# Half-size seven-product blocks in two feed-forward up phases, and split parts of the hidden tensors made in the down phases

## The reference

```python
def swiglu_ffn(x, w_in, w_out):            # feed-forward 0 and 1
    gate, up = jnp.split(x @ w_in, 2, axis=-1)
    return (jax.nn.silu(gate) * up) @ w_out
...
def conv_ffn(x, w_up, conv_w, conv_b, w_down):   # feed-forward 2 and 3
    up = x @ w_up
    a, g = up[..., :D_FF_2], up[..., D_FF_2:]
    g = causal_dwconv(g, conv_w) + conv_b
    return (jax.nn.gelu(g) * a) @ w_down
```

## Time and profile before

| what | value |
|---|---|
| median of three runs | 2401.6 us |
| the profiled execution | 2402.46 us |
| its span, first to last instruction | 2400.6 us |
| mean granted TensorE clock | 0.998 of 2.4 GHz |
| PE busy | 2385.5 us (99%) |
| DVE, ACT, POOL busy | 1094.6, 806.7, 65.3 us |
| DMA engines, mean share | 27.7% |

### The profile page before, as it was taken

The page is one execution under the profiler, slowest core; times in us unless marked ns, Lnnn a source line. Parts: engine busy times, 40 slices in busy tenths (PEclk is TensorE's granted clock), DMA queues, the critical chain, the costliest instruction groups (busy, mean ns, idle before and its releaser), DMA issues.

```text
span 2400.6 us, 27033 instructions
## 1 busy us (share of the span) xinstructions
PE 2385.5 (99%) x12158; PEld 2026.4 (84%) x12158; DVE 1094.6 (46%) x1040; ACT 806.7 (34%) x891; POOL 65.3 (3%) x39
## 2 busy tenths in 40 slices
PE   9999999999999999999999999999999999999998
PEld 8888889898788888898987888888888977888887
DVE  4333225574553332256735544424545546544424
ACT  4222225455542222233432433322322432333311
POOL 0000000230100000000000000000000000000000
PEclk9999999999999999999999999999999999999999
DMA  4223323212132223142521222231432511222321
GB/s 163 103 91 105 106 88 126 76 37 88 39 120 90 104 90 112 70 164 87 177 73 56 103 101 95 98 115 66 153 106 72 191 70 71 88 105 88 122 90 68
DMA packets 34691, 238.30 MB, mean 99 GB/s; under 512 B 4108, under 2 KB 4492, under 8 KB 6800
## 3 DMA queue, kind: packets, MB, share of 16 engines
q1 hardware_dynamic: 34432, 236.56, 27.7%
q10 hardware_dynamic: 144, 0.00, 0.0%
HBM read 234.46 MB, written 2.10 MB: 99 GB/s over the span
## 4 chain that ended last, share of the span: by engine, by line
PE 98%; DVE 1%; ACT 1%; issue 0%; DMA 0%; DVEq 0%
PE bank L452 55%; PE bank L526 28%; PE bank L491 4%; PE bank L873 4%; PE bank L514 1%; PE bank L900 1%; PE bank L727 1%; PE bank L920 1%; PE bank L659 0%; PE bank L669 0%; PE bank L567 0%; DVE xn L1545 0%; PE bank L628 0%; PE bank L911 0%; PE bank L654 0%
## 5 line engine op out<-in xcount | busy, mean ns | idle before, releaser
L452 PE MATMUL bank<-a_hi,w_hi 128*128 128x512 f32 (+1 forms) x2112 | 787.2, 373 | 0.4 <-DVE a_lo L1590 0.4
L452 PE MATMUL bank<-a_hi,w_lo 128*128 128x512 f32 (+1 forms) x2112 | 782.8, 371 | 0.0
L452 PE MATMUL bank<-a_lo,w_hi 128*128 128x512 f32 (+1 forms) x2112 | 782.8, 371 | 0.0
L1520 DVE TENSOR_TENSOR w_lo<-raw,w_hi 128x2048 fp32r<-128x2048 f32 x207 | 476.5, 2302 | 502.3 <-ACT w_hi L1043 501.8
L1043 ACT ACTIVATE w_hi<-raw 128x2048 fp32r<-128x2048 f32 x207 | 394.5, 1906 | 357.2 <-DMA raw<-w_full 357.2
L452 PEld LDWEIGHTS bank<-a_hi,w_hi 128*128 128x128 f32 x2112 | 398.8, 189 | 69.9 <-issue 1.7
L452 PEld LDWEIGHTS bank<-a_hi,w_lo 128*128 128x128 f32 x2112 | 398.7, 189 | 67.7 <-issue 0.7
L452 PEld LDWEIGHTS bank<-a_lo,w_hi 128*128 128x128 f32 x2112 | 398.6, 189 | 67.1
L526 PE MATMUL bank<-w_hi,h_hi 128*128 128x512 f32 x692 | 270.1, 390 | 0.0
L526 PE MATMUL bank<-w_hi,h_lo 128*128 128x512 f32 x692 | 269.6, 390 | 0.0
L526 PE MATMUL bank<-w_lo,h_hi 128*128 128x512 f32 x692 | 269.6, 390 | 0.0
(11 more groups left out here) (297 smaller groups left out, 2320.1 us busy)
## 6 DMA issues: line engine op xcount, KB each, us to landing
raw<-w_full SPq DMA_DIRECT2D x207, 1024.0 KB, 4.8
rows_ab<-rows SPq DMA_DIRECT2D x8, 1024.0 KB, 5.4
x<-x SPq DMA_DIRECT2D x4, 512.0 KB, 6.4
mem_raw<-mem SPq DMA_DIRECT2D x2, 1024.0 KB, 8.2
out<-x SPq DMA_DIRECT2D x3, 512.0 KB, 2.6
raw<-w_full SPq DMA_DIRECT2D x2, 512.0 KB, 6.3
...
```

The costliest lines, as they stand in the source:

```text
L452: last = mm(bank[:, b + m, cols], w[:, s, c0:c0 + P], act_in[:, k, cols], start=(k == 0 and j == 0), stop=(k == KD - 1 and j == 2))
L1520: V.tensor_tensor(w_lo[:, u % SLOTS, :], raw[:, u % SLOTS, :], w_hi[:, u % SLOTS, :], ALU.subtract).then_inc(w_split, 1)
```

## The change

In units 5 to 20 of `up0` and `up1` the weights (two tiles by eight blocks) are seen as 2 x 2 blocks: gate or up tile, and first or second half of the contraction. The activations are seen as 2 x 2 blocks too: half of the contraction, and early or late 256 tokens. Eight block products become seven, of sums and differences of blocks. Each of the seven is 12 matmuls of 256 columns (`seven_unit`). GpSimd forms four sums of activation blocks once a phase (`token_sums`, `t1` to `t4`) and four sums of weight blocks for each unit (`first_weight_sum` in place in `raw`, `rest_weight_sums` into `s23_raw`, `s4_raw`). ScalarE and VectorE split these sums as they split the weights. Each product goes to half a bank, two sets of four banks alternate, and VectorE adds the products up into gate and up tile (`seven_results`), after ScalarE has copied the first product to SBUF (`copy_first`), which the seventh waits for. The weights of unit n+2 are split in the pass of unit n in these units.

In all four layers `h32` now holds all 22 hidden tiles in float32, and no high or low part is made in the up phase beside the last two units. `hidden_high` and `hidden_low` make them two tiles at a time (128 x 1024) into four stages as the down phase goes (`down_parts`). The down phase's first unit takes the token tiles in the order 2, 0, 1, 3 in layers 0 and 1. SyncE's loads of the gain rows wait for unit 20 in place of the last hidden tile. Three sets of semaphores become one.

```diff
+SEVEN0, SEVEN1 = 5, 21
+SEVENS = [range(SEVEN0, SEVEN1), range(SEVEN0, SEVEN1), (), ()]
+NTH_SEVEN = {fu: n for n, fu in enumerate((f, u) for f in range(4) for u in SEVENS[f])}
...
+        def stage_free(f, u):
+
+            if u < SLOTS:
+                return gemm_done, gemm_at(f"up{f}", SEVEN1 - 1)
+            return out_used, USED0[f"down{f}"] + u - SLOTS + 1
...
+            def token_sums(f, which):
...
+                t1, t2, t3, t4 = (t_raw[:, n, :, :] for n in range(4))
+                if which == 1:
+                    (h2, l2), (h1, l1) = b(0, 1), b(0, 0)
...
+                ins.then_inc(t_sum, 1)
...
+            def first_weight_sum(f, u):
...
+                gp.wait_ge(w_loaded[g % SLOTS], 16 * (g // SLOTS + 1))
+                G.tensor_tensor(w[:, 2 * QS:3 * QS], w[:, 2 * QS:3 * QS], w[:, 3 * QS:4 * QS],
+                                ALU.add).then_inc(first_sum, 1)
+
+            def rest_weight_sums(f, u):
...
+                gp.wait_ge(first_sum, j + 1)
+                step = 2 if f >= 2 else 1
+                if u - 2 * step >= SEVEN0:
+                    gp.wait_ge(gemm_done, gemm_at(f"up{f}", u - 2 * step, 0))
+                link(G.tensor_tensor(s2, w[:, 2 * QS:3 * QS], w[:, 0:QS], ALU.subtract))
+                G.tensor_tensor(s3, w[:, 3 * QS:4 * QS], s2, ALU.subtract)
+                G.tensor_tensor(s4, w[:, QS:2 * QS], s2, ALU.subtract).then_inc(rest_sums, 1)
...
+                gp.wait_ge(a_lo_tok, TURN0[UP_GEN[f]] + NT)
+                for which in (1, 3, 2, 4):
+                    token_sums(f, which)
+                first_weight_sum(f, SEVEN0)
+                for u in SEVENS[f]:
+                    rest_weight_sums(f, u)
+                    if u != SEVENS[f][-1]:
+                        first_weight_sum(f, u + (2 if f >= 2 else 1))
...
+            def seven_unit(f, u):
...
+                def product(dst, half, weights, c0, moving):
+                    (hi, lo), (m_high, m_low) = weights, moving
+                    for k in range(KD // 2):
+                        for i, (st, mv) in enumerate(((hi, m_high), (lo, m_high), (hi, m_low))):
+                            last = mm(bank[:, dst, 256 * half:256 * half + 256], st[:, c0 + k * P:c0 + k * P + P], mv[:, k, :],
+                                      start=(k == 0 and i == 0), stop=(k == KD // 2 - 1 and i == 2))
+                    return last
...
+                pe.wait_ge(w_split, U0[name] + u + 1)
+                bank_wait(name, u)
+                product(b, 0, w, 0, b_block(0, 0)).then_inc(first_product, 1)
+                product(b + 1, 0, w, QS, b_block(1, 0))
+                pe.wait_ge(t_split, 4 * f + 2)
+                product(b + 2, 1, w, 2 * QS, t_block(1))
+                pe.wait_ge(s_split, j + 1)
+                product(b + 2, 0, s23, QS, t_block(3))
+                product(b + 3, 1, s4, 0, b_block(1, 1))
+                pe.wait_ge(t_split, 4 * f + 4)
+                product(b + 1, 1, s23, 0, t_block(2)).then_inc(gemm_done, 1)
+                pe.wait_ge(first_copied, j + 1)
+                product(b, 1, w, 3 * QS, t_block(4)).then_inc(gemm_done, 1)
...
-                    pe.wait_ge(h_done, F0[f] + 2 * u + 2)
-                    for t in (2, 3, 0, 1):
-                        if u == 0 and t == 0:
+                    pe.wait_ge(h_split, n * f + u + 1)
+                    order, early, late = ((2, 0, 1, 3), 0, 3) if f < 2 else ((2, 3, 0, 1), 0, 1)
...
                         last = part(u, t)
...
+            def copy_first(f, u):
+
+                act.wait_ge(first_product, NTH_SEVEN[f, u] + 1)
+                S.activation(h32[:, u, 0:256], bank[:, up_bank(f, u), 0:256], ACT.Copy).then_inc(first_copied, 1)
+
+            def hidden_high(f, u):
+                act.wait_ge(*hidden_at(f, 2 * u + 1))
+                act.wait_ge(*stage_free(f, u))
+                S.activation(h_hi[:, stage(u), :], h32[:, 2 * u:2 * u + 2, :], ACT.Copy).then_inc(h_high, 1)
...
+                    if is_seven(f, n + 1):
+                        copy_first(f, n + 1)
+                    if n + 3 == SEVEN0 and SEVENS[f]:
+                        for i, k in enumerate((0, 2, 1, 3)):
+                            act.wait_ge(t_sum, 4 * f + i + 1)
+                            S.activation(t_hi[:, k, :, :], t_raw[:, k, :, :], ACT.Copy).then_inc(t_high, 1)
+                    if n + 3 < SEVEN0 or not SEVENS[f]:
+                        split_upto(U0[name] + n + 3)
+                    elif n + 2 >= SEVEN0:
+                        split_upto(U0[name] + n + 2 + (n >= SEVEN1 - 1))
+                    if n >= SEVEN1 - 1:
+                        hidden_high(f, n - SEVEN1 + 1)
...
+            def down_parts(f):
+
+                name = f"down{f}"
+                for u in range(KF - SEVEN1 + 1, UNITS[name]):
+                    hidden_high(f, u)
+                    split_upto(U0[name] + u + 1)
...
+                    if unit_of(u) is not None:
+                        dve.wait_ge(rest_sums, unit_of(u) + 1)
                     V.tensor_tensor(w_lo[:, u % SLOTS, :], raw[:, u % SLOTS, :], w_hi[:, u % SLOTS, :],
...
+            def low_sums(f, u):
...
+                dve.wait_ge(s_high, j + 1)
+                V.tensor_tensor(s23_lo[:, j % 2, :], s23_raw[:, j % 2, :], s23_hi[:, j % 2, :], ALU.subtract)
+                V.tensor_tensor(s4_lo[:, j % 2, :], s4_raw[:, j % 2, :], s4_hi[:, j % 2, :],
+                                ALU.subtract).then_inc(s_split, 1)
...
+            def hidden_low(f, u):
+                dve.wait_ge(h_high, UNITS["down0"] * f + u + 1)
+                V.tensor_tensor(h_lo[:, stage(u), :], h32[:, 2 * u:2 * u + 2, :], h_hi[:, stage(u), :],
+                                ALU.subtract).then_inc(h_split, 1)
...
+            def seven_results(f, u):
...
+                link(V.tensor_tensor(gate_c[:, :].rearrange("p (n c) -> p n c", n=2),
+                                     h32[:, u:u + 1, early].broadcast_to([P, 2, 256]), half_banks(b + 1), ALU.add))
+                link(V.tensor_tensor(h2, gate_c[:, late].unsqueeze(1).broadcast_to([P, 2, 256]), half_banks(b + 2), ALU.add))
+                V.tensor_tensor(gate_c[:, late], h32[:, u, late], bank[:, b + 3, late], ALU.add).then_inc(gate_ready, 1)
+                dve.wait_ge(gate_ready, NTH_SEVEN[f, u] + 1)
+                link(V.tensor_tensor(h32[:, u, late], h32[:, u, early], bank[:, b + 2, late], ALU.add))
+                dve.wait_ge(gemm_done, gemm_at(name, u))
+                V.tensor_tensor(h32[:, u, early], h32[:, u, early], bank[:, b, late], ALU.add).then_inc(ffn_banks, 1)
...
+                    if is_seven(f, n + 2):
+                        split_upto(U0[name] + n + 2)
...
+                    if is_seven(f, n):
+                        dve.wait_ge(ffn_banks, F0[f] + n + 1)
+                        V.tensor_tensor(h32[:, n, :], gate_s[:, s, :], h32[:, n, :], ALU.mult).then_inc(h_done, 1)
+                    else:
+                        dve.wait_ge(gemm_done, gemm_at(name, n))
+                        V.tensor_tensor(h32[:, n, :], gate_s[:, s, :], bank[:, b + 1, :], ALU.mult).then_inc(ffn_banks, 1)
+                    if is_seven(f, n + 2):
+                        low_sums(f, n + 2)
```

253 lines of the change are left out of this document (197 added, 56 removed).

## The result

The changed kernel takes 2371.73 us, the median of four runs (2370.91 to 2372.62). The kernel before takes 2401.57 us (2399.81 to 2401.78). The ratio is 0.9877, with a 95% interval of 0.9860 to 0.9895: 1.2% faster, 29.8 us. The profiled execution took 2372.62 us, its span 2370.8 us.

A forecast was written before the change was run, and what follows sets the result against it. TensorE's matmuls were taken to bound the kernel. 32 units at 0.94 us less each give 30 us, other edits nothing: 2402.46 - 30 = 2372.5 us profiled, about 2372 for the median, range 2362 to 2388.

The forecast's parts named there:

- The rate: TensorE in the 32 units of seven products: 9.94 us a unit, 0.94 less than before, 30 us in all.
- as memory units 0 to 3 do: Products three and seven move `t_hi`, `t_lo` from the low arena against the weights, so 0.1177 us a matmul.
- Rival (a): All 256-column matmuls of the seven-product units run at 0.1200 us: 2376 us; chance 0.15.
- Rival (b): Matmuls run at 0.1134 us wherever sums take part in the seven-product units: 2363 us; chance 0.05.
- (e): Smaller matmuls keep their rate but something else ends the up phases, so no gain shows; chance 0.03.
- With 3.8 us the least cover.: In seven-product units TensorE never waits: `w_lo` ends at 16.1 us and is wanted at 19.9.
- With VectorE's splits between them they end by 56: Phase start: GpSimd's ten activation sums, from 28 us on, end by 56, leaving 7 us of cover before unit 5.
- this doesn't pile up: the start of `w_lo` is set by GpSimd, and VectorE's work of a unit is 7.5 of 9.94 us: VectorE's queue in seven-product units: low parts of the sums are 0.2 us late, but lateness doesn't grow.
- Rival (c): GpSimd and VectorE block each other at every step: 11.1 us a seven-product unit, 2410 us; chance 0.09.
- Above 11.4 us from sixth product to `w_lo` TensorE starts to wait, above 13.2 slower than before: Limits for the chain over GpSimd to `w_lo` in seven-product units, reckoned at 7.6 us.
- The down tails: Unit 8 of each down phase: `h_lo` ready 0.6 us ahead in `down0`, 0.4 in `down2`; nothing counted, at most 3 us.
- Rival (d): TensorE waits in part, through dependent sums, half-bank additions or down tails: half the gain lost, 2387 us; chance 0.13.

The follow-up runs named there:

- the stages without the sevens: Changed kernel with no unit by seven products, everything else of the change kept: 2401.23 us, ratio 0.9996 to the kernel before.
- the aligned kernel: Changed kernel with token sums `t_hi` and `t_raw`/`t_lo` at KB 50 and 66, not 50.3125 and 66.3125: 2373.93 us in a single run.
- the kernel with other operands: Changed kernel with all seven products moving `a_hi`, `a_lo` against `w_hi`, `w_lo`, sums made but not used: 2375.1 us, ratio 0.9888 to the kernel before.

## Why the prediction was right

**The rate (2372, measured 2371.73).** The step "60 x 0.1177 = 7.06, and 9.94 us a unit" was right in size: 9.946 measured, 0.93 less than 10.88, times 32. That the other edits cost nothing was right (the stages without the sevens: 2401.23). The reason given for 0.1177 was half wrong, and that the size held was in part luck. Choosing it "as memory units 0 to 3 do", since they too read the low arena, took the region for the cause; the aligned kernel keeps the region and gives 0.1200 for `t`. In the changed kernel `t_hi` happens to lie at a like offset to the memory tensor's (50.3125 and 64.3125 KB). For products four to six 0.1177 was a middle with no row behind it. Rival (a), 0.1200 everywhere, is what the kernel with other operands gave (2375.1 us against 2376 worked out), 3.4 us above the changed kernel. Rival (b) asked for 0.1134, and (e) for another bound, and the trace has neither.

**"With 3.8 us the least cover."** As a duration it was right (3.9 us), and the order of events was right to a few tenths: sums beside PSUM additions, `w_lo` at 3.3 us. As a statement of safety it was wrong twice. First, the start had 2.0 us and not 7. The step "With VectorE's splits between them they end by 56" put too little on the splits: the ten sums of 128 x 1024 took 2.40 us each where nothing stood beside them, but 3.2 on average from 28.1 to 60.4 us. Second, the binding margin is VectorE's queue. The prediction put it aside with "this doesn't pile up: the start of `w_lo` is set by GpSimd, and VectorE's work of a unit is 7.5 of 9.94 us". It is 8.4, with `w_lo` blocked, and its three other two-input operations cost 3.3 more as soon as they meet GpSimd's. 11.7 against 9.95 us piles up in one unit.

**Rival (c).** "Above 11.4 us from sixth product to `w_lo` TensorE starts to wait, above 13.2 slower than before" was a threshold of the wrong quantity. One more sum, 1.3 us on top of a chain of 7.4 (7.6 worked out), already costs 14.6 us, and two make the kernel 0.8% slower than before. The mechanism, GpSimd and VectorE blocking each other, was the right one; it needs no doubled price on all sums, and it lies 1.3 us away. That the changed kernel stayed clear of it was luck as far as the prediction goes: nothing in it worked out this distance, so its 0.09 had no measure behind it.

**The down tails.** In `down0` and `down2` 0.8 us of cover where 0.6 and 0.4 were worked out, and no wait of TensorE in any of the four. Rival (d) had nothing to show.

What stays open: why the offset of an operand changes TensorE's rate, and whether the blocked pattern, once entered from outside, would be left by itself in the changed kernel. Its first unit starts in it (the sums' low parts take 1.72 and 1.78 us at 71.3) and the second is free of it, so there is some power to recover; how much was not tried.
